# Expert layer with token-major sums: VectorE multiplies, ScalarE sums, weights computed after a step of routing

## The reference

```python
q = (hb @ peer_wq).reshape(B, Q_BLOCK, PEER_HEADS, 2, PEER_HALF)        # 8 heads, 2 halves of 128
s = jnp.einsum('bqhpd,hpnd->bqhpn', q, peer_subkeys)                     # 128 scores a half
vals, idx = lax.top_k(s, PEER_TOPK)                                      # best 16 of each half
combo = vals[..., 0, :, None] + vals[..., 1, None, :]                    # 256 pairs
top_s, pos = lax.top_k(combo, PEER_TOPK)                                 # best 16 pairs = 16 experts
g = jax.nn.softmax(top_s, axis=-1)
a = jax.nn.gelu(jnp.einsum('bqhkd,bqd->bqhk', u_sel, hb))                # dot product with row u of each expert
return jnp.einsum('bqhk,bqhkd->bqd', g * a, v_sel)                       # weighted sum of the rows v
```

## Time and profile before

| | |
|---|---|
| median of 3 runs | 1173.74 us (1173.55 to 1173.74) |
| the profiled execution | 1174.32 us, its span 1172.5 us |
| granted TensorE clock, mean | 0.971 |
| busy: TensorE matmul, weight load | 1048.3 us (89%), 978.6 us (83%) |
| busy: VectorE, ScalarE, GpSimd | 838.1 us (71%), 429.7 us (37%), 269.9 us (23%) |
| gathered by the indirect DMAs | 268.45 MB of 390.35 MB |
| dot products on VectorE (line 2070) | 256 of 1.22 us, and 256 read-outs of 0.08 us |
| products of line 1576 | 4096 records, mean 0.28 to 0.29 us |
| GELU of pieces (line 1146) | 359.0 us of ScalarE's idle time lie ahead of it |

### The profile page before, as it was taken

One profiled execution on the slowest core, in us unless ns is written; L12 is line 12 of the kernel. 1 busy time (PEld: TensorE's weight loads), 2 busy tenths in 40 slices (PEclk: granted clock), 3 DMA queues, 4 the chain that ended last, 5 costly groups with the idle time before them and its releaser, 6 DMA issues.

```text
span 1172.5 us, 18875 instructions
## 1 busy us (share of the span) xinstructions
PE 1048.3 (89%) x7587; PEld 978.6 (83%) x7587; DVE 838.1 (71%) x1802; ACT 429.7 (37%) x905; POOL 269.9 (23%) x289
## 2 busy tenths in 40 slices
PE   7999997999999988777787778878999999999997
PEld 6999986998899887677787777778999888898885
DVE  6998987667567667666777766655665868775776
ACT  3636732123212221222132122211457554476452
POOL 2001004343334333333333333434000000300000
PEclk9999998999999999999899999989999999999999
DMA  9986858999999999999999999999865655455540
GB/s 370 407 329 226 349 191 330 420 421 421 420 421 420 421 420 421 420 421 421 420 421 420 420 421 422 420 421 420 340 221 176 229 202 180 158 202 180 194 165 36
DMA packets 59576, 390.35 MB, mean 333 GB/s; under 512 B 6881, under 2 KB 7905, under 8 KB 15714
## 3 DMA queue, kind: packets, MB, share of 16 engines
q0 software_dynamic: 36864, 268.45, 55.1%
q1 hardware_dynamic: 21152, 120.10, 27.6%
q10 hardware_dynamic: 1474, 0.60, 0.2%
HBM read 388.08 MB, written 1.05 MB: 332 GB/s over the span
## 4 chain that ended last, share of the span: by engine, by line
PE 62%; DMA 25%; DVE 7%; ACT 4%; issue 1%; SPq 0%; ACTq 0%; DVEq 0%
PE aux L1576 23%; DMA rows<-in_peer_uv,work 23%; PE pj L1619 6%; PE pj L1620 6%; PE pj L1621 6%; PE pj L1293 5%; PE pj L1295 5%; PE pj L1294 5%; PE aux L1552 4%; DVE rows L2070 2%; DVE rows L1767 1%; DMA rows<-in_w_ada 1%; ACT work L1152 1%; ACT rows L1019 1%; PE aux L1432 1%
## 5 line engine op out<-in xcount | busy, mean ns | idle before, releaser
L1576 PE MATMUL aux<-work,rows 128*128 128x128 f32 x2080 | 261.0, 289 | 73.7 <-ACT work L1152 73.7
L1576 PEld LDWEIGHTS aux<-work,rows 128*128 128x128 f32 x2080 | 253.8, 204 | 81.4 <-ACT work L1152 81.0
L1576 PE MATMUL aux<-work,low_pairs 128*128 128x128 f32 x2016 | 237.7, 279 | 31.0 <-ACT work L1152 31.0
L1576 PEld LDWEIGHTS aux<-work,low_pairs 128*128 128x128 f32 x2016 | 232.8, 195 | 34.5 <-ACT work L1152 34.5
L908 POOL DMA_INDIRECT rows<-in_peer_uv,work x130 | 122.8, 945 | 297.8 <-PE aux L1576 230.3
L715 DVE TENSOR_TENSOR wlo<-wring,whi 128x1024 fp32r<-128x1024 f32 x98 | 118.5, 1235 | 76.8 <-ACT whi L709 76.3
L908 POOL DMA_INDIRECT low_pairs<-in_peer_uv,work x126 | 118.7, 942 | 158.9 <-PE aux L1576 154.2
L1293 PE MATMUL pj<-xh,whi 128*128 128x256 f32 x512 | 146.9, 287 | 0.3 <-DVE wlo L647 0.2
L1146 ACT ACTIVATE work<-work 128x4 f32<-128x4 f32 (+2 forms) x71 | 14.7, 207 | 359.0 <-DVE work L2070 359.0
L1295 PE MATMUL pj<-xh,wlo 128*128 128x256 f32 x512 | 145.4, 284 | 0.0
L1294 PE MATMUL pj<-xl,whi 128*128 128x256 f32 x512 | 145.4, 284 | 0.0
(11 more groups left out here) (290 smaller groups left out, 1475.6 us busy)
## 6 DMA issues: line engine op xcount, KB each, us to landing
wring<-in_w SPq DMA_DIRECT2D x76, 1024.0 KB, 4.9
rows<-in_w_ada SPq DMA_DIRECT2D x46, 512.0 KB, 9.2
rows<-in_w SPq DMA_DIRECT2D x3, 1024.0 KB, 11.2
rows<-in_peer_uv,work POOLq DMA_INDIRECT x130, 17.3
work<-in_late_rows SPq DMA_DIRECT2D x2, 1024.0 KB, 8.5
xT<-in_gate_rows SPq DMA_DIRECT2D x2, 1024.0 KB, 7.0
rows<-in_norm_rows SPq DMA_DIRECT2D x2, 1024.0 KB, 7.2
low_pairs<-in_peer_uv,work POOLq DMA_INDIRECT x126, 18.1
```

The source lines that it names most:

```text
L1576: ins = mm(peer_sum[t][:, c * P:(c + 1) * P], pair(n)[:, D + c * P:D + (c + 1) * P], diag[:, n % PICKS, :], start=(n % (EXPERT_HEADS * PIC ...
```

## The change

1. `dot` on VectorE is a plain multiplication (`tensor_tensor`) for all groups but the last; it writes the products over the row u. ScalarE adds them up with a copy that has an accumulator, four in a row at the head of each piece, and raises `dotted`. The last group keeps the old instruction.
2. `sum_pair` on TensorE is token-major for all groups but the last: the diagonal is the stationary side and 512 columns of v the moving one, two matmuls a pick. The last group keeps the eight turned matmuls.
3. The sum of a tile, being token-major, is turned: ScalarE copies it to `hT` (`sum_to_turn`, after piece 1 of group 8 for tile 0 and after piece 0 of the last group for tile 1), TensorE multiplies it with the identity (`turn_sum`, ahead of group 9 and after pick 4 of the last group) into `turned_sum`, banks 2 and 3, on top of which the last group adds for tile 1.
4. `weigh` on VectorE stands behind the routing step of its piece, in groups 0 to 13.

```diff
+        turned_sum = peer_sum[0]
...
+            def sum_to_turn(t, rows_summed):
+
+                act.wait_ge(pair_used, rows_summed)
+                for c in range(2):
+                    nc.scalar.copy(quarter(hT, t, c), by_chunk(peer_sum[t][:, half(c)])).then_inc(sum_out, 1)
+
             for g in range(NT * EXPERT_HEADS):
                 for k, (first, size) in enumerate(groups_of(g)):
                     some = slice(first, first + size)
-                    act.wait_ge(dotted, g * PICKS + first + size)
+                    if g < LAST_GROUP:
+                        for j in range(first, first + size):
+                            n = g * PICKS + j
+                            act.wait_ge(multiplied, n + 1)
+                            nc.scalar.activation(pair(n)[:, 0:D], pair(n)[:, 0:D], ACT.Copy, accum_out=dots[g % 2][:, j:j + 1]).then_inc(dotted, 1)
+                        act.wait_ge(dotted, g * PICKS + first + size)
+                    else:
+                        act.wait_ge(last_dotted, first + size)
...
+                    if g == EXPERT_HEADS and k == 1:
+                        sum_to_turn(0, EXPERT_HEADS * PICKS)
+                    if g == LAST_GROUP and k == 0:
+                        sum_to_turn(1, LAST_GROUP * PICKS)
...
+                if n < LAST_GROUP * PICKS:
+                    for c in range(2):
+                        ins = mm(peer_sum[t][:, half(c)], diag[:, n % PICKS, :], pair(n)[:, D + c * 512:D + (c + 1) * 512],
+                                 start=(n % (EXPERT_HEADS * PICKS) == 0), stop=False, skip_group_check=True)
+                else:
+                    if n == LAST_GROUP * PICKS:
+                        pe.wait_ge(x_ready, KC)
+                    for c in range(KC):
+                        ins = mm(turned_sum[:, c * P:(c + 1) * P], pair(n)[:, D + c * P:D + (c + 1) * P], diag[:, n % PICKS, :],
+                                 start=(n == LAST_GROUP * PICKS and c % 4 == 0), stop=False, skip_group_check=True)
+                ins.then_inc(pair_used, 1)
+
+            def turn_sum(t):
+
                 for c in range(KC):
-                    ins = mm(peer_sum[t][:, c * P:(c + 1) * P], pair(n)[:, D + c * P:D + (c + 1) * P], diag[:, n % PICKS, :],
-                             start=(n % (EXPERT_HEADS * PICKS) == 0 and c % 4 == 0), stop=False, skip_group_check=True)
-                ins.then_inc(pair_used, 1)
+                    pe.wait_ge(sum_out, 2 * t + c // 4 + 1)
+                    ins = mm(turned_sum[:, c * P:(c + 1) * P], hT[:, c, tile_of(t)], ident[:, :],
+                             start=(t == 0 and c % 4 == 0), stop=False, skip_group_check=True)
+                ins.then_inc(sum_turned, 1)
...
+                if g == EXPERT_HEADS + 1:
+                    turn_sum(0)
...
+                        if g == LAST_GROUP and j == 4:
+                            turn_sum(1)
...
-                v.tensor_tensor_reduce(row, row, h2_tok[g // EXPERT_HEADS], 1.0, 0.0, ALU.mult, ALU.add,
-                                       dots[g % 2][:, j:j + 1]).then_inc(dotted, 1)
+                if g < LAST_GROUP:
+                    v.tensor_tensor(row, row, h2_tok[g // EXPERT_HEADS], ALU.mult).then_inc(multiplied, 1)
+                else:
+                    v.tensor_tensor_reduce(row, row, h2_tok[g // EXPERT_HEADS], 1.0, 0.0, ALU.mult, ALU.add,
+                                           dots[g % 2][:, j:j + 1]).then_inc(last_dotted, 1)
...
-                    weigh(g, k, first, size)
+                    if nxt >= NT * EXPERT_HEADS:
+                        weigh(g, k, first, size)
...
                         if k == 2:
                             route_experts(nxt)
+                        weigh(g, k, first, size)
...
                 if g == EXPERT_HEADS + 1:
-                    dve.wait_ge(pair_used, EXPERT_HEADS * PICKS)
+                    dve.wait_ge(sum_turned, 1)
                     join(0)
```

More of the change, by code:

```diff
@@ L538, in build @@
             sem("routed"), sem("gate_exp"), sem("dotted"), sem("dots_act"), sem("weighted"), sem("diag_ready"))
+        multiplied, last_dotted = sem("multiplied"), sem("last_dotted")
         pair_loaded = [sem(f"pair_loaded{s}") for s in range(SLOTS)]
         pair_used = sem("pair_used")
+        sum_out, sum_turned = sem("sum_out"), sem("sum_turned")
         single_gates, single_diag = sem("single_gates"), sem("single_diag")
@@ L2092, in join @@
                     x = xT[:, c, t * P:(t + 1) * P]
-                    v.scalar_tensor_tensor(x, peer_sum[t][:, c * P:(c + 1) * P], mod[:, 5 * KC + c:5 * KC + c + 1], x, ALU.mult, ALU.add) \
+                    v.scalar_tensor_tensor(x, turned_sum[:, c * P:(c + 1) * P], mod[:, 5 * KC + c:5 * KC + c + 1], x, ALU.mult, ALU.add) \
                         .then_inc(x_ready, 1)
```

## The result

The changed kernel takes 1228.72 us (median of 4 runs, 1226.21 to 1228.80), the kernel before 1173.74: 55.0 us or 4.6% slower, ratio 1.0459 with a 95% interval of 1.0447 to 1.0472. The forecast was 1228.

A forecast was written before the change was run, and what follows sets the result against it. Two equally long loops, TensorE's chain and the DMA, bound groups 0 to 4, the DMA alone later. 1174.3 plus 53.4 later landings and 1.8 turning gave 1229.5, 1228.9 against the median; it said 1228, range 1208 to 1243.

The forecast's parts named there:

- The loop: Groups 0 to 4: sums behind ScalarE's copies stretch the period from 39.66 to 49.5 us, 51.7 with the slow clock.
- rival D: Token-major products: 512-column records take 0.85 us, a pick 3.4, a group 54 everywhere; over 1380 us; 1%.
- The price of a sum: One ScalarE sum over 128x1024 costs 1.05 us, bounds 1.0 and 1.24; four cost 4.2 us.
- Rival C: Sums on ScalarE cost 1.24 us each, 2.3 us more a group over 5 groups: 1240 us; 13%.
- The clock: TensorE's new idle stretches ahead of pieces 2 and 3 halve its clock; piece 2 takes 2.2 us more, piece 3's is hidden.
- rival B: As forecast, but TensorE keeps its clock: period 49.5 us, time 1216 us; 14%.
- Everything behind moves by what the DMA lost: After group 4, the fourth gather of a piece lands at 473.4 instead of 420.00 us; everything behind moves by 53.4.
- the slots: Twelve gather slots, 30 us of DMA, only shift a phase; each microsecond added to TensorE's early loop is lost.
- the turning at the end: Turning tile 1's sum in the last group, between picks 4 and 5 on TensorE, adds 1.8 us at the end.
- Weights behind routing: VectorE routes before the weights, up to 2.9 us per piece; in groups 5 to 13 only slots are held longer.
- The table load: GELU's 1.28 us load on ScalarE stands behind piece 0's sums; no 1.38 us drain, with which time would be 1235.
- Rival A: DMA alone sets the early loop and covers the added 9.9 us: 1175 to 1176 us, no change; 5%.

The follow-up runs named there:

- Gaps filled: The changed kernel with TensorE's idle stretches behind queries and keys in groups 0 to 4 filled by products of a zero matrix: 1218.6 us, ratio 1.0374.
- Copies behind: The changed kernel with ScalarE's query copies moved behind the whole of piece 2 and the score copy behind piece 3: 1172.9 us, ratio 0.9989.
- Order alone: The kernel before with one edit, the weights behind the routing step: 1174.4 us, ratio 1.0002.
- Matmuls alone: Token-major products and turned sums only, with dots on VectorE and weights before routing as in the kernel before: 1174.9 us, ratio 1.0011.
- Copies behind, tile 1 turned: The changed kernel with the query and score copies moved behind pieces 2 and 3, and tile 1's products turned as before: 1172.5 us, ratio 0.9984.
- Early groups on VectorE: The changed kernel, but groups 0 to 4 keep VectorE's old dot product, multiply and sum in one: 1174.5 us, ratio 1.0005.
- Weights first: The changed kernel with the weights ahead of the routing step, as in the kernel before: 1233.2 us, ratio 1.0505.

## Why the prediction was right

**The loop.** The mechanism and its place were as predicted. With the start of the queries as zero, in the group shown above:

| step | predicted, full clock | predicted with the clock | after |
|---|---|---|---|
| piece 2 starts | 12.4 | 12.4 | 12.6 |
| keys | 19.3 | 21.5 | 21.1 |
| piece 3 | 26.1 | 28.3 | 27.9 |
| piece 1 | 42.7 | 44.9 | 44.5 |
| next queries | 49.5 | 51.7 | 51.5 |

The last piece 3 of the early groups starts at 456.73 (predicted 455.7). The mean period is 52.1 (predicted 51.7). The step from piece 3 to piece 0, predicted as 9.05 us and hidden here by the slow piece 3, shows in "Gaps filled": 296.64 to 305.67, 9.03. A token-major pick at full clock takes 1.72 us (piece 2 of "Copies behind", 265.38 to 272.25), the value taken, so rival D is out.

**The price of a sum.** 1.04 to 1.06 us, next start 1.04 later, its read-out in the overlap: the value taken. Where VectorE's products set the pace it is one per 1.13 us. Rival C, with 1.24, is out.

**The clock.** In the stretch 220 to 430 the granted clock is 0.89, and 8.5 to 10.1 us for the pieces behind idle stretches of 5.6 to 5.8 us, in place of 6.9, is 1.6 to 3.2 us of it. The 2.2 taken lies in between. "Gaps filled" shows the price on the chip, 10 us of 55; rival B, for which TensorE keeps its clock, would have been 1216 and is out.

**Everything behind moves by what the DMA lost.** Predicted 53.4 us for all landings after group 4. The last pick's dot product, which waits for its landing, is at

```profile
887.30 1.22 DVE L2112 CUSTOM_DVE_ANT_0 rows<-rows,aux 128x1024 f32<-128x1024 f32 x1 [0.44 <-DMA rows<-in_peer_uv,work]
```

in the kernel after, and in the kernel before at

```profile
832.99 1.22 DVE L2070 CUSTOM_DVE_ANT_0 rows<-rows,aux 128x1024 f32<-128x1024 f32 x1 [0.52 <-DMA rows<-in_peer_uv,work]
```

so 54.3 us, and the span is longer by 54.4.

**Too strong in words, right in the sum: the slots.** The prediction opens with two loops of which neither has a tenth of a microsecond to give, and calls each microsecond added to the first one lost. "Order alone" adds 0.6 us to each of its turns and loses nothing. The sum did allow for it, by letting a gather land 6.4 us after its issue, where landings from 400 us on had taken 15 or more: the last early piece 3 starts 60.8 us later than before (456.73 against 395.91), the gathers 54.3.

**Wrong by its size: the turning at the end.** 1.8 us was to be added; 54.4 less 54.3 leaves 0.1. The two terms erred in opposite directions, by 0.9 and 1.7 us. TensorE at the last group, in the kernel after:

```profile
849.73 8.83 PE L1597 MATMUL aux<-low_pairs,work 128*128 128x512 f32 x16 [2.79 <-ACT work L1168]
858.53 9.20 PE L1603 MATMUL aux<-work,rows 128*128 128x128 f32 x80
867.57 1.95 PE L1611 MATMUL aux<-ident,hT 128*128 128x128 f32 x16
```

Five picks in 9.0 us, 1.80 each, where the first six of the earlier trace rows took 12.6, 2.1 each. The slow clock fell on the last group before and falls on the piece ahead of it now; this makes up for the 1.8 us of turning. That it does so exactly is read from the traces, not tested: "Matmuls alone", which has the turning too, lost 0.2 to 2.5 us, and "Copies behind, tile 1 turned", which leaves the turning out, is only 0.4 us below "Copies behind".

**Weights behind routing.** Predicted as a part of the new loop (piece 1 7.5 us after piece 0) and free in groups 5 to 13. Both hold: the weights of pieces 0 and 1 are at 308.18 and 315.74, and "Early groups on VectorE" keeps the new order and loses nothing. That the old order would be worse still, since VectorE would wait for ScalarE ahead of its routing, the prediction didn't say; "Weights first" shows it.

**The table load.** Row and page disagreed on a drain of 1.38 us per switch. In the kernel after, the load at 306.57 begins 0.01 after the read-out ends and GELU begins 0.02 after the load; nothing is there for a drain of this size. The row was right, and the Trainium skill's "ScalarE: Activation LUTs", on what a table load costs, doesn't hold for this sequence.

**Rival A** named what decides it, whether the added time lies beside the chain. "Copies behind" is that rival made true by moving two copies: the same work, and no loss.

## What to carry to other kernels

Before work is moved to an engine that is idle a third of the time, look at what it stands waiting for in program order, and whether the moved work would come behind that wait: here the same 240 sums cost 55 us while 40 of them stand behind two copies, and 2.3 us or nothing with those 40 ahead of them. When two loops are equally long, moving work into one of them costs its full price per turn, less what buffers absorb once; shortening one gains nothing. And prices of single places don't add when each also moves an idle stretch and with it the clock.

## What the runs showed that was not expected

- The twelve slots absorb more than was thought. A loop of 40.3 us in the early groups cost 0.4 us or nothing, loops of 41.7 us 2.3 to 3.3 us, although the DMA's own pace is 39.8; the landings show where it is taken. In 240 to 380 us the kernel before and "Order alone" have

```profile
DMA to landing us min/median/max: 9.7/13.4/19.2
...
DMA to landing us min/median/max: 7.1/10.4/15.8
```

  in that order: the time from issue to landing shrinks by 3 us, while the rate falls only from 420 to 417 GB/s.
- The clock's cost is not bound to one gap. Kept busy ahead of pieces 2 and 3, TensorE fell to the slow clock at piece 0, after an idle stretch of only 1.90 us. Nor does the length of the stretch alone decide it: in "Copies behind" 1.96 us of idle came ahead of 282.13, and the piece ran at a clock of 1.00 in 7.13 us; the same 1.96 us came ahead of 321.54, and the piece took 8.83 us at a clock of 0.53 to 0.61.
